# A decoder step on one core: the per-head normalisation and the sample recurrence, as stages of their own or inside the routing loop

## The reference, cut to what matters

```
# one step of the sample group, per sequence and head: S is 64 x 64
sa = einsum('bhij,bhj->bhi', S, a)
S  = S * w[..., None, :] + sa[..., None] * b[..., None, :] + v[..., None] * k[..., None, :]
y  = einsum('bhij,bhj->bhi', S, r)
# both groups: group norm over the 64 channels of each head, then bonus, gate, output product
ym = y.mean(-1); yv = square(y - ym).mean(-1)
y  = ((y - ym) * rsqrt(yv + GN_EPS)).reshape(B, T, D) * lnx_g + lnx_b
out = ((y + bonus) * g) @ w_o
# then, for each token
x = layer_norm(alpha * x + gate(c) * out);  h = x * (1 + scale(c)) + shift(c)
logits = h @ router_w        # top-2 of 32 experts in the best group, then the experts
```

## Time and profile before

| | us |
|---|---|
| median of 3 runs | 4775.69 |
| lowest, highest run | 4762.6, 7678.84 |
| the profiled execution's own time | 4760.31 |
| its span, first to last instruction | 4758.6 |

### The profile page before, as it was taken

How to read it: one execution, slowest core, us unless ns; L and a number is a source line. 1 busy time by engine, 2 the same in 40 slices (tenths; PEclk the granted TensorE clock), 3 DMA queues, 4 the chain that set the end, 5 groups by cost and what they waited for, 6 DMA issues and landing times. The chain is left out here.

```text
span 4758.6 us, 62928 instructions
## 1 busy us (share of the span) xinstructions
PE 3725.3 (78%) x25854; PEld 2203.2 (46%) x25854; DVE 1482.4 (31%) x2834; ACT 733.0 (15%) x1252; POOL 702.2 (15%) x454
## 2 busy tenths in 40 slices
PE   5399985888843665999998098996785938999991
PEld 1166644878732332444443044554774424444440
DVE  0310104666656341111111632002554931111116
ACT  0000112322201000111110100012453200111112
POOL 0000013323222211000000400000441320000004
PEclk9699987998966887999999589998887969999995
DMA  9952121111114417888886621216545328888874
GB/s 399 366 195 80 67 105 65 56 66 35 44 49 154 139 53 303 329 339 329 339 332 243 236 76 49 71 58 121 153 101 154 110 97 341 328 339 330 339 303 177
DMA packets 335329, 888.92 MB, mean 187 GB/s; under 512 B 68468, under 2 KB 138372, under 8 KB 329373
## 3 DMA queue, kind: packets, MB, share of 16 engines
q1 hardware_dynamic: 282064, 687.64, 41.0%
q0 software_dynamic: 39648, 151.87, 8.0%
q10 hardware_dynamic: 13392, 46.13, 2.4%
HBM read 701.23 MB, written 188.56 MB: 187 GB/s over the span
## 5 line engine op out<-in xcount | busy, mean ns | idle before, releaser
L1912 PE MATMUL moe_ps_h<-moe_wi,moe_xT 128*128 128x512 f32 x2112 | 922.3, 595 | 18.6 <-DMA moe_wi<-in_moe_w_in_dram 18.6
L1912 PEld LDWEIGHTS moe_ps_h<-moe_wi,moe_xT 128*128 128x128 f32 x2112 | 397.9, 191 | 495.9 <-issue 495.9
L1931 PE MATMUL moe_ps_y<-moe_wo,moe_hT 128*128 128x512 f32 x1056 | 464.1, 592 | 0.0
L2376 PE MATMUL qkv_ps<-qkv_hh,qkv_wr 128*128 128x512 f32 (+1 forms) x1152 | 382.5, 489 | 22.1 <-DVE qkv_qsT L2326 19.6
L394 PE MATMUL mix_ps<-mix_mix,mix_wr 128*128 128x344 f32 x1152 | 334.8, 454 | 22.0 <-issue 22.0
L1989 DVE TENSOR_TENSOR moe_h<-moe_sg,moe_ps_h 128x512 f32<-128x512 f32 x66 | 45.4, 687 | 914.4 <-PE moe_ps_h L1912 914.4
L1931 PEld LDWEIGHTS moe_ps_y<-moe_wo,moe_hT 128*128 128x128 f32 x1056 | 195.5, 190 | 221.0 <-issue 221.0
L1756 PE MATMUL post_ps_mm<-post_wo,post_zt 128*128 128x512 f32 x576 | 261.9, 615 | 38.5 <-DMA post_wo<-in_rwkv_w_o_dram 35.9
L2376 PEld LDWEIGHTS qkv_ps<-qkv_hh,qkv_wr 128*128 128x128 f32 x1152 | 193.2, 194 | 211.7 <-issue 188.7
L394 PEld LDWEIGHTS mix_ps<-mix_mix,mix_wr 128*128 128x128 f32 x1152 | 219.6, 191 | 136.8 <-issue 23.2
L1882 POOL DMA_DIRECT2D moe_X<-t_xs_d x66 | 34.8, 528 | 1393.9 <-PE moe_ps_x L1893 1377.5
(11 more groups left out here) (390 smaller groups left out, 5008.4 us busy)
## 6 DMA issues: line engine op xcount, KB each, us to landing
moe_wi<-in_moe_w_in_dram SPq DMA_DIRECT2D x66, 4096.0 KB, 16.1
moe_wo<-in_moe_w_out_dram SPq DMA_DIRECT2D x66, 2048.0 KB, 13.4
ada_w<-in_ada_w_dram SPq DMA_DIRECT2D x32, 1536.0 KB, 36.5
moe_X<-t_xs_d POOLq DMA_DIRECT2D x70, 512.0 KB, 8.0
t_ysl_d<-moe_y ACTq DMA_DIRECT2D x68, 512.0 KB, 7.9
t_xs_d<-mix_z POOLq DMA_DIRECT2D x1, 25600.0 KB
t_proj_d<-mix_ev POOLq DMA_DIRECT2D x48, 516.0 KB
wkv_raw<-t_proj_d SPq DMA_DIRECT2D x40, 516.0 KB
```

The costliest lines, as they stand in the source:

```text
L1912: ins = pe.matmul(ps_h[:, half], xT[:, j, k, :], wi[:, j, k, half * DE:(half + 1) * DE], start=(k == 0), stop=(k == KC - 1))
L1931: ins = pe.matmul(ps_y[:, half], hT[:, k, :], wo[:, 1 - j, k, half * 512:(half + 1) * 512], start=(k == 0), stop=(k == KE - 1))
L2376: ins = pe.matmul(ps[n % 2][:, s, 0:w], wr[:, n % 4, k, :], hh[:, 0, k, s * 512:s * 512 + w], start=(k == 0), stop=(k == KC - 1))
```

## The change

The stages `phase_sample` and `phase_gn` are gone; their work is in `phase_post` of layer 0.

- The recurrence now makes its output with tokens on partitions. Slab 3 leaves the `MV` steps; two steps `v` (after `S10` and `S11`) compute it with the operands' roles exchanged, ScalarE copies each in one piece of 512 columns, and the `y` steps (now after `S13` and `S15`) do the same for their part. `y0` waits for the copy of `v1`, `y1` for VectorE's addition of `y0`. `Y` goes to a `y_d` of 1024 token rows in pieces of 512 bytes.
- In layer 0's loop VectorE normalises tile t+3 (`gsum`, `gmean`, `gc`, then after ScalarE's `gq` the steps `gvar`, `geps`, `grs`, `gz`). TensorE turns it (`zh0`, `zh1`), ScalarE copies it in eight pieces of 128x128 with the norm's weight and bias (`zc`), and VectorE adds the bonus and multiplies by the gate in place (`zb`, `zg`) for tile t+2.
- The sample step is cut in 8 pieces of 128x512: three GpSimd products (`pa`, `pw`, `pv`) and six VectorE operations (`ua` to `uy`) each. Four pieces run before tile 0, after `s_k`, and one behind each of tiles 0 to 3. The state lies in `xm[:, 4:8]`, so GpSimd waits with tile 4 until it is stored.
- SyncE loads `y` rows, bonus and gate by tile. In its order the loads for tile 7 stand behind the stores of the sample state, which wait for piece 7.

```diff
         if n in (0, 4, 8):
             back += [("MV", n // 4 + 1)]
-        if n in (11, 15):
+        if n in (10, 11):
+            back += [("v", n - 10)]
+        if n in (13, 15):
             back += [("y", n // 15)]
...
-                        sp.dma_start(T["y_d"][(i - 1) * P:i * P, 0:NP], Y[:]).then_inc(s_y, 16)
+                        sp.dma_start(T["y_d"][0:NP, (i - 1) * P:i * P].rearrange("(t p) n -> p t n", p=P), Y[:]).then_inc(s_y, 16)
...
+                def group_mean(t):
+                    dve.wait_ge(s_y[t % 3], 16 * (t // 3 + 1))
+                    if t:
+                        dv_.wait(dve, f"gc{t - 1}")
+                    dv_.step(f"gsum{t}", dve.tensor_reduce(gs[:, 0], heads(z[:, t % 3]), AX, ALU.add))
+                    dv_.wait(dve, f"gsum{t}")
+                    dv_.step(f"gmean{t}", dve.tensor_scalar(gs[:, 0], gs[:, 0], 1.0 / HD, None, ALU.mult))
...
+                    dv_.step(f"gc{t}", dve.tensor_tensor(zj, zj, wide(gs[:, 0], HD), ALU.subtract))
...
+                    dv_.step(f"gvar{t}", dve.tensor_reduce(gs[:, 1], heads(square), AX, ALU.add))
...
+                    dv_.step(f"geps{t}", dve.tensor_scalar(gs[:, 1], gs[:, 1], 1.0 / HD, GN_EPS, ALU.mult, ALU.add))
+                    ac_.wait(dve, f"gsd{t}")
+                    dv_.step(f"grs{t}", dve.reciprocal(gs[:, 1], gs[:, 1]))
...
+                    dv_.step(f"gz{t}", dve.tensor_tensor(zj, zj, wide(gs[:, 1], HD), ALU.mult))
...
+                def gated(t):
+                    dve.wait_ge(s_bg, 32 * (t + 1))
+                    ac_.wait(dve, f"zc1{t}")
+                    dv_.step(f"zb{t}", dve.tensor_tensor(zt[:, t % 2], zt[:, t % 2], bg[:, 0], ALU.add))
+                    dv_.wait(dve, f"zb{t}")
+                    dv_.step(f"zg{t}", dve.tensor_tensor(zt[:, t % 2], zt[:, t % 2], bg[:, 1], ALU.mult))
...
+                    po_.wait(dve, f"pv{c}")
+                    op("ua", dve.tensor_reduce(sa[:], u, AX, ALU.add))
+                    op("ub", dve.tensor_tensor(u, val(sa[:]), key(sv[:, 5]), ALU.mult))
+                    op("ut", dve.tensor_tensor(u, u, sT[:, c % 2, 1], ALU.add))
+                    op("us", dve.tensor_tensor(x, x, u, ALU.add))
+                    op("um", dve.tensor_tensor(u, x, key(sv[:, 0]), ALU.mult))
+                    op("uy", dve.tensor_reduce(sy[:, 8 * c:8 * c + 8], u, AX, ALU.add))
...
+                    group_mean(0)
+                    group_mean(1)
+                    group_scale(0)
+                    group_mean(2)
+                    group_scale(1)
+                    gated(0)
+                    group_scale(2)
+                    gated(1)
                 dve.wait_ge(s_k, NK)
...
+                if not layer:
+                    for c in range(SFIRST):
+                        sample_step(c)
                 for t in range(TT):
...
+                    if normed(t + AHEAD):
+                        group_mean(t + AHEAD)
                     pe_.wait(dve, f"mm{t}")
...
+                    if normed(t + AHEAD):
+                        group_scale(t + AHEAD)
+                    if normed(t + 2):
+                        gated(t + 2)
+                    if chunk(t):
+                        sample_step(SFIRST + t)
...
+                    po_.step(f"pa{c}", pool.tensor_tensor(sT[:, c % 2, 0], x, key(sv[:, 4]), ALU.mult))
...
+                    po_.step(f"pw{c}", pool.tensor_tensor(x, x, key(sv[:, 1]), ALU.mult))
+                    po_.step(f"pv{c}", pool.tensor_tensor(sT[:, c % 2, 1], val(sv[:, 3, 8 * c:8 * c + 8]), key(sv[:, 2]), ALU.mult))
...
+                    if normed(t) and t == SCH - SFIRST:
+                        dv_.wait(sp, f"us{SCH - 1}")
+                        sp.dma_start(T["wkv_sample"], state).then_inc(s_So, 16)
+                        dv_.wait(sp, f"uy{SCH - 1}")
+                        sp.dma_start(T["ys_d"].rearrange("s (h d) -> (s h) d", d=HD), sy[:]).then_inc(s_ys, 16)
+                    if normed(t + 3):
+                        y_tile(t + 3)
+                    if normed(t + 2):
+                        bonus_gate(t + 2)
...
                 for t in range(TT):
+                    if turned(t + 2):
+                        zturn(0, t + 2)
                     if t + 1 < TT:
-                        product(t + 1)
-                    if more:
-                        zturn(0, t + 2)
+                        product(t + 1, 0)
+                    if turned(t + 2):
+                        zturn(1, t + 2)
+                    if t + 1 < TT:
+                        product(t + 1, 1)
...
-    phase_sample(nc, T)
-    phase_gn(nc, T)
     phase_post(nc, T, 0)
```

More of the change, by code:

```diff
@@ L1061, in _ @@
                         pe_.step(f"S{n}.{c}", ins)
+                    elif k == "v":
+                        x = s[2]
+                        dv_.wait(pe, f"N3.{c}")
+                        for u in range(8 * x, 8 * x + 8):
+                            o = (u % 8) * CH
+                            for q in range(2):
+                                pe.matmul(ps[half(q), 6 + x, o:o + HD], GK[half(q), b, u, 1, :], tokV[half(q), b, u, :], start=True, stop=False)
+                            for q in range(2):
+                                ins = pe.matmul(ps[half(q), 6 + x, o:o + HD], GB[half(q), b, u, 1, :], PQ[half(q), u, 1, :], start=False, stop=True)
+                        pe_.step(f"v{x}.{c}", ins)
                     elif k == "y":
@@ L1400, in phase_post @@
         combined = lambda t: layer == 1 and t < TILES
+        normed = lambda t: layer == 0 and t < TT
+        turned = lambda t: t < TT
+        SFIRST, SCH = 4, HD // 8
+        chunk = lambda t: layer == 0 and SFIRST + t < SCH
         MIX = ("cmin", "csub", "cl", "csum", "crcp", "cw", "c0", "c2", "ca", "cz")
+        G1, G2 = ("gsum", "gmean", "gc"), ("gvar", "geps", "grs", "gz")
+        SMP = ("ua", "ub", "ut", "us", "um", "uy")
         NORM = ("gmul", "res", "st0", "st1", "ag", "eps", "rs", "xn", "xg", "x1")
-        names = [f"{n}{t}" for t in range(AHEAD) if combined(t) for n in MIX]
+        if layer:
+            names = [f"{n}{t}" for t in range(AHEAD) for n in MIX]
+        else:
+            names = [f"{n}{t}" for group, t in ((G1, 0), (G1, 1), (G2, 0), (G1, 2), (G2, 1), (("zb", "zg"), 0), (G2, 2), (("zb", "zg"), 1)) for n in group]
+            names += [f"{n}{c}" for c in range(SFIRST) for n in SMP]
@@ L1408, in phase_post @@
         for t in range(TT):
-            more = layer == 1 and t + 2 < TT
-            names += [f"mm{t + 1}"] * (t + 1 < TT) + [f"zh0{t + 2}"] * more + [f"tr{t}"] + [f"zh1{t + 2}"] * more + [f"lg{t}"]
+            names += [f"zh0{t + 2}"] * turned(t + 2) + [f"zh1{t + 2}"] * turned(t + 2) + [f"mm{t + 1}"] * (t + 1 < TT) + [f"tr{t}", f"lg{t}"]
         pe_ = Seq(A.sem("pe_steps"), names)
-        names = ["aexp0", "aexp1"] + [f"zc{h}{t}" for t in range(2) for h in range(2)] + ["aexp2"] if layer else []
+        zc = lambda t: [f"zc0{t}", f"zc1{t}"]
@@ L1512, in _ @@
                 pool.wait_ge(s_k, NK)
+                if not layer:
+                    pool.wait_ge(s_S, 16)
+                    for c in range(SFIRST):
+                        sample_products(c)
                 for t in range(TT):
@@ L1604, in _ @@
+                if layer:
+                    for t in range(AHEAD):
+                        mix(t)
+                else:
+                    group_mean(0)
[6 more added lines that the diff above has]
+                    gated(1)
                 dve.wait_ge(s_k, NK)
                 link(dve.tensor_scalar(down[:], iota[:, 0:EG], -1.0, float(EG), ALU.mult, ALU.add))
+                if not layer:
+                    for c in range(SFIRST):
+                        sample_step(c)
@@ L1760, in _, with product @@
-                if layer:
-                    pe.wait_ge(s_k, NK)
-                    for t in range(2):
-                        zturn(0, t)
-                        zturn(1, t)
-                product(0)
+                def product(t, b):
+                    if b == 0:
+                        if layer:
+                            ac_.wait(pe, f"zc1{t}")
+                        else:
+                            dv_.wait(pe, f"zg{t}")
+                        if t >= 2:
+                            dv_.wait(pe, f"gmul{t - 2}")
+                    if t == 0:
+                        pe.wait_ge(s_wo[b], 16)
+                    for k in range(KC):
+                        ins = pe.matmul(ps_mm[:, t % 2, b], zt[:, t % 2, k, :], wo[:, k, b * 512:(b + 1) * 512],
+                                        start=(k == 0), stop=(k == KC - 1))
+                    if b:
+                        pe_.step(f"mm{t}", ins)
@@ L1766, in _ @@
+                pe.wait_ge(s_id, NID)
+                for t in range(2):
+                    zturn(0, t)
+                    zturn(1, t)
+                product(0, 0)
+                product(0, 1)
                 pe.wait_ge(s_k, NK)
                 for t in range(TT):
```

(11 more changed lines are left out.)

414 lines of the change are left out of this document (154 added, 260 removed).

## The result

The kernel after takes **4645.05 us** (median of 4 runs, 4634.06 to 4649.02), the kernel before 4775.69 in the same job. The ratio is 0.9729, 95% interval 0.9698 to 0.976: faster by 2.7%. The forecast was 4656 with a range of 4608 to 4705. Three executions that lie far above the others of their kernel (7678.84 and 4888.99 of before, 9998.91 of `early_pieces`) are left out of every median and ratio here.

A forecast was written before the change was run, and what follows sets the result against it. Two serial stages without TensorE work precede a TensorE-bound routing stage with 83 us of free VectorE time. Removing 198.4, adding 89.7 and 1, saves 107.7: 4652.6 from the profiled 4760.3, 4656 for the median; range 4608 to 4705.

The forecast's parts named there:

- Removed, 198.4: Sample and group norm stages, serial before the routing stage: all 198.4 us go, first loads, barriers and memory trips included.
- The start: Start of the routing stage: constants at 43 us, four sample pieces in 24, first layer norm at 74.8 instead of 28.3.
- the rival with both at their upper bounds: Routing stage: GpSimd products of 1.63 and 1.40, constants at 49, last layer norm at 276.9, kernel 4668 us; chance 0.10.
- Tiles 0 to 3: Routing loop: VectorE, not TensorE, sets the pace at 26.8 us a tile, 107.3 for four.
- nothing collides: Routing stage: GpSimd works only beside VectorE's reductions and waits; tiles of 23.3 us, kernel 4628; chance 0.17.
- The wait at tile 4: Routing loop: VectorE stands about 8.4 us for tile 7's rows, loaded behind the sample state's stores; bounds 3 and 9.
- Tiles 4 to 8: Later routing tiles: intervals of 19.3, 16.7, 16.7 and 18.0 us, the later ones set by TensorE's output product.
- that rival: Routing loop: TensorE's clock stays low, a tile takes 36.3 us on TensorE, kernel 4738; chance 0.07.
- The recurrence, the step that failed: Recurrence: as many products as before, so TensorE's work stays and the change is 0 us, bounds -8 and +10.
- a period other than 66.5: Recurrence: a chunk takes 66.5 us; any other period was named as a sign of being wrong.
- The rival on the other side, a recurrence that loses its overlap to the new waits: Recurrence: new waits of v and y lengthen each chunk; at 20 us per chunk the kernel takes 4813; chance 0.04.
- The last store, +1: End of the recurrence: the last store, then in pieces of 512 bytes, costs 1 us more; bounds 0 and 3.5.

The follow-up runs named there:

- early_pieces: The kernel after, with GpSimd's first sample products waiting only for the state and its vectors, and two pieces done before tile 1's gating: 4639.92 us.
- rec_only: The kernel before with only the recurrence of the kernel after, its sample, group norm and routing stages kept: 4753.21 us, ratio 0.9965.
- v_both: The kernel after, with the second v step moved next to the first, so both stand ahead of TensorE's longest wait in a chunk: 4627.78 us.

## Why the prediction was right, and the step that failed

**Removed, 198.4.** Right as a balance term. The stage starts at 1364.55, not at 1373: 19.6 less in the recurrence, 11.8 more ahead of it.

**The start.** `zg0` ended at 30.6 (forecast 35.8), constants were there at about 39 (43), `zg1` ended at 45.9 (45.6), since it waited for tile 1's bonus and gate, and not for VectorE. The four pieces took 21.7 instead of 24 and no lead for GpSimd: it had worked ahead in VectorE's wait. First layer norm at 71.4, forecast 74.8. The stage's 12.2 MB came in 39 us, 313 GB/s, and a product of GpSimd took 1.26 alone; the rival with both at their upper bounds is out.

**Tiles 0 to 3.** Forecast 26.8, measured 26.25. The line of operations from `x1` to `pv` that exclude each other was 11.9 in the forecast and is 11.15. The rival *nothing collides* (23.3) is refuted three ways by the experiments. The Trainium skill (SBUF — State Buffer, SBUF: two separate sides) calls the shared pair of interfaces an exclusive lock: whichever of a GpSimd operation and a VectorE operation in a 2-port mode or with two SBUF inputs starts first has it for its whole length. The rows above agree to about 0.15 us, also for the one-input copy (2.30 against 0.16) and tensor_scalar (1.29 against 0.17), which my working had left out: I had taken two-input operations alone.

**The wait at tile 4.** Forecast 8.4, measured 7.77, by the mechanism named.

**Tiles 4 to 8.** Forecast 19.3, 16.7, 16.7 and 18.0; measured 18.87, 17.40, 20.30 and 19.48, 5.4 more in sum. Some halves of TensorE's output product took 8.6 to 8.7 us instead of 7.03, and behind a wait of 10.81 us for `xm` of tile 4 the transposes and the router took 1.97 and 3.62, which is the lower clock. The longer halves were to be seen before: the loop of before has output products of 13.98 and of 15.68 us and tiles 17.77 and 19.47 apart, and the sum took 13.98 for all. The difference is the granted clock: 0.80 to 0.81 over the longer halves (0.80 in 1689.27 to 1697.90 before, 0.81 in 1569.00 to 1577.40 after), 1.00 over the short ones. Why it falls in every second tile or so was not tested. The lower clock was there in tiles 0 to 3 too, but unlike in that rival not throughout (granted 0.74 in the loop), and VectorE's 26.25 covered it. Errors of both signs left the stage's sum, 260.2, within 1 us of the forecast's 261.2.

**The recurrence, the step that failed.** "I take 0, bounds -8 and +10." It gave -19.6 in the profile and -17.1 in rec_only. I had counted products and found the same number, and had not asked who waited for the moved products where they were, and in which wait they would land. The chunk of before has one wait of 4.5 us in which TensorE has nothing, and behind it a stretch at a lower clock. Of the 19.6, 9.3 are the difference in waits for XB over the stage (31.8 and 22.5), 4.3 TensorE's busy time (536.34 and 532.08), the rest small waits that I did not separate. From the first y store to the sixth a chunk takes 74.6 us before (903.14 to 1275.96) and 71.0 after (913.41 to 1268.38). The 66.5 us of the prediction is a mean over seven chunks, of which the last two are shorter (59.9 and 32.5); taken the same way it is 63.8 after, (1359.95 - 913.41) / 7, and a period other than 66.5 was one of the signs that I had named for being wrong. The rival on the other side, a recurrence that loses its overlap to the new waits, is refuted with the sign reversed: TensorE has no wait of 0.3 us or more at a `v` or `y` step.

**The last store, +1.** It landed after 3.4 us instead of 2.8; from its issue to the next stage's first issue it is 4.60 instead of 3.99.

**The total.** The sum gave -107.7 and the profiles differ by 111.3, but that closeness is partly luck: the missing -19.6 is offset by +18.0 in untouched code, of which the profile of before had the short variant. In the medians, where such things average out, the difference is 131 us, 23 more than the sum, and the recurrence is most of it.

## What to carry to other kernels

When an edit moves work without changing its amount, look up the longest wait of the engine it moves on, and ask on which side of it the work lands and whether the engine waited for still needs it. Do not sum VectorE's and GpSimd's busy times apart: put the VectorE operations with two SBUF inputs, its copies and tensor_scalars, and GpSimd's operations in one line, and lay GpSimd's beside reductions, PSUM readers and waits. A tiny instruction with a long row is worth a look at what ends at the same moment on the other engine.

## What the runs showed of the hardware that was not expected

A VectorE copy of 128x16 from SBUF took 2.30 us beside a GpSimd product and a reduction over the same operand 0.16. A tensor_scalar of 128x16 took 1.29 beside GpSimd and 0.17 alone, one of 128x8 1.23 (L1574, ending at 1411.57 where `pw` ends at 1411.54), while the reciprocal of 128x16 (0.25) and the reduction of 1024 elements (1.21) stayed as they were. When both engines compete, GpSimd's rows lengthen as well: 2.25 for a product of 1.27. And TensorE's clock behind its wait for XB, granted over the next 3 us: 0.50 to 0.54 behind all seven waits of 4.47 to 4.93 us in before, 0.50 or 0.51 behind four and 1.00 behind two of the six waits of 2.9 us in after, 1.00 behind all six of 0.9 to 1.2 us in v_both.
